# Two 256-column matmuls with the same weights become one of 512 columns, in four stages of a two-block layer

## The reference

```python
# first block
h = rmsnorm(x, norm_mix);  p = h @ w_in
x = x + concat(pool(p), hyena(p), gating(p)) @ w_out          # w_out 2048 x 2048
h = rmsnorm(x, norm_ffn)
up = dwconv3(h @ ffn_w_up, ffn_conv_w, ffn_conv_b)            # 2048 x 11264, width-3 convolution over tokens
gate, val = split(up);  x = x + (silu(gate) * val) @ ffn_w_down   # 5632 x 2048
x = rmsnorm(x, norm_final)
# second block
proj = rms_norm(x) @ w_in_2                                   # attention, RWKV-7, memory attention
merged = sigmoid(ga)*(ya @ w_up_a) + sigmoid(gb)*(yb @ w_up_b) + sigmoid(gc)*(yc @ w_up_c)
return x + merged @ w_o                                       # w_o 2048 x 2048
```

## Time and profile before

| | |
|---|---|
| median of 3 runs | 2539.17 us (2537.14 to 2540.28) |
| span of the profiled execution | 2537.8 us; its own whole time is not listed apart, the median lies 1.4 us above this span |
| mean granted TensorE clock | 0.985 of full speed |
| TensorE busy | 2455.0 us, 97% |
| weight loads busy | 2413.6 us, 95% |
| VectorE busy | 1534.1 us, 60% |
| ScalarE busy | 1185.9 us, 47% |
| DMA | 400.39 MB, mean 158 GB/s |

### The profile page before, as it was taken

How to read it: one execution, slowest core, us unless ns; L and a number is a source line. 1 busy time by engine, 2 the same in 40 slices (tenths; PEclk the granted TensorE clock), 3 DMA queues, 4 the chain that set the end, 5 groups by cost and what they waited for, 6 DMA issues and landing times.

```text
span 2537.8 us, 51128 instructions
## 1 busy us (share of the span) xinstructions
PE 2455.0 (97%) x19960; PEld 2413.6 (95%) x19960; DVE 1534.1 (60%) x2050; ACT 1185.9 (47%) x1502; POOL 12.8 (1%) x27
## 2 busy tenths in 40 slices
PE   6999998999999999997899999999999999999999
PEld 6898997999999999996899999999999999999999
DVE  6456566666555666566866666766576454544454
ACT  5343335665434666434444445444465443434433
POOL 0000000000000000000000000000000000000000
PEclk9999898999999999998999999999999999999999
DMA  6353354555554555554333333333355355555554
GB/s 233 130 180 116 129 187 132 188 170 194 183 186 167 183 181 189 179 185 147 117 119 112 109 120 111 119 123 104 118 175 173 125 184 179 185 176 175 184 187 160
DMA packets 110145, 400.39 MB, mean 158 GB/s; under 512 B 12394, under 2 KB 12421, under 8 KB 109904
## 3 DMA queue, kind: packets, MB, share of 16 engines
q1 hardware_dynamic: 108000, 391.00, 46.4%
q0 software_dynamic: 2032, 7.67, 0.9%
HBM read 396.52 MB, written 2.10 MB: 157 GB/s over the span
## 4 chain that ended last, share of the span: by engine, by line
PE 92%; DVE 5%; issue 1%; ACT 1%; DMA 0%; DVEq 0%; SPq 0%; ACTq 0%
PE bank L417 91%; DVE w_lo L1316 1%; ACT w_hi L909 1%; DVE scratch L1365 1%; PE bank L611 0%; DVE s_k L1365 0%; DVE h_lo L1362 0%; DMA x<-in_xT 0%; DVE cum L1362 0%; DVE root L1404 0%; DVE ping L1362 0%; DVE s_t L1362 0%; DVE qr L1807 0%; DVE acc L1362 0%; DVE s_t L1369 0%
## 5 line engine op out<-in xcount | busy, mean ns | idle before, releaser
L1316 DVE TENSOR_TENSOR w_lo<-raw,w_hi 128x1024 fp32r<-128x1024 f32 x736 | 892.0, 1224 | 803.8 <-ACT w_hi L909 797.5
L909 ACT ACTIVATE w_hi<-raw 128x1024 fp32r<-128x1024 f32 x736 | 770.7, 1057 | 1018.7 <-PE bank L417 999.5
L417 PE MATMUL bank<-h_hi,w_hi 128*128 128x256 f32 x4016 | 1163.3, 290 | 36.6 <-DVE h_lo L1362 15.0
L417 PE MATMUL bank<-h_lo,w_hi 128*128 128x256 f32 x4016 | 1141.0, 284 | 0.0
L417 PE MATMUL bank<-h_hi,w_lo 128*128 128x256 f32 x4016 | 1140.8, 284 | 0.0
L417 PEld LDWEIGHTS bank<-h_hi,w_hi 128*128 128x128 f32 x4016 | 775.6, 193 | 47.0 <-issue 24.4
L417 PEld LDWEIGHTS bank<-h_lo,w_hi 128*128 128x128 f32 x4016 | 775.9, 193 | 3.3 <-issue 2.2
L417 PEld LDWEIGHTS bank<-h_hi,w_lo 128*128 128x128 f32 x4016 | 775.0, 193 | 0.0
L417 PE MATMUL bank<-m_hi,w_lo 128*128 128x256 f32 x704 | 197.8, 281 | 0.0
L417 PE MATMUL bank<-m_hi,w_hi 128*128 128x256 f32 x704 | 197.1, 280 | 0.0
L417 PE MATMUL bank<-m_lo,w_hi 128*128 128x256 f32 x704 | 195.7, 278 | 0.0
(11 more groups left out here) (414 smaller groups left out, 2820.2 us busy)
## 6 DMA issues: line engine op xcount, KB each, us to landing
raw<-in_units SPq DMA_DIRECT2D x736, 512.0 KB, 3.4
x<-in_xT SPq DMA_DIRECT2D x4, 512.0 KB, 5.8
memx<-in_memT POOLq DMA_DIRECT2D x4, 512.0 KB, 7.2
out_y<-obuf SPq DMA_DIRECT2D x8, 256.0 KB, 4.3
bias_t<-in_bias POOLq DMA_DIRECT2D x8, 192.0 KB, 2.9
dft<-in_dft POOLq DMA_DIRECT2D x1, 1024.0 KB, 7.6
decay<-in_decay POOLq DMA_DIRECT2D x1, 768.0 KB, 5.6
con<-in_con SPq DMA_DIRECT2D x1, 546.0 KB, 7.8
```

What stands on the lines that cost most here:

```text
L417: return pe.matmul(out, lhsT, rhs, start=start, stop=stop, skip_group_check=True)
L909: return act.activation(out, in_, ACT.Copy, scale=scale)
L1316: dve.tensor_tensor(w_lo[slot][:, :, :], raw[slot][:, :, :], w_hi[slot][:, :, :].bitcast(F32), ALU.subtract).then_inc(split_done, 1)
```

## The change

In the four stages the high and the low half of an activation now lie in one tensor ("both", with an index 0 or 1 ahead of the tile index). TensorE streams both halves, 512 columns, in one matmul with w_hi into a whole bank: 256 columns of w_hi·hi beside 256 columns of w_hi·lo. The w_lo·hi product, 256 columns, is added into the first half of the bank. A triple becomes a pair. An output tile now fills a bank, a group two banks ("wide"), and all eight banks serve as four wide ones. Whoever evicts has to add the two halves of each bank. As wide group 0 covers banks 0 and 1, and wide group 1 banks 2 and 3, TensorE waits ahead of w_out and ahead of w_o until banks 0 and 1 have both been read.

```diff
-        banks = [ctx.enter_context(nc.psum_tensor(f"bank{i}", [P, 512], F32)) for i in range(8)]
+        wide = [ctx.enter_context(nc.psum_tensor(f"wide{i}", [P, 2, 2 * T], F32)) for i in range(4)]
+        banks = [wide[i // 2][:, i % 2, :] for i in range(8)]
...
+        h_both = sb("h_both", [P, 2, KT, T], F32R)
+        h_hi, h_lo = h_both[:, 0], h_both[:, 1]
...
+        def part_of(b, s):
+            return WIDE[b][:, :, s * T:(s + 1) * T]
...
+            def wide_unit(bank, k0, both, first, last):
+                slot = next(slots) % RING
+                pe.wait_ge(split_done, n.next("split"))
+                for kk in range(UK):
+                    for t in range(2):
+                        o = WIDE[bank][:, t, :]
+                        mm(o, w_hi[slot][:, kk, t * P:(t + 1) * P], both[:, :, k0 + kk, :], first and kk == 0, False)
+                        m = mm(o[:, 0:T], w_lo[slot][:, kk, t * P:(t + 1) * P], both[:, 0, k0 + kk, :], False,
+                               last and kk == UK - 1)
+                m.then_inc(unit_used, 1)
...
+            for b in (0, 1):
+                pe.wait_ge(bank_read[b], n.now(("fill", b)))
             with n.loop(4, {("fill", 0): 1, ("fill", 1): 1, "split": 8}):
-                group(1, y_hi, y_lo, ready=(dve_for_pe, (most, most, most, rest)))
-                group(0, y_hi, y_lo)
+                wide_group(1, y_both, ready=(dve_for_pe, (most, most, most, rest)))
+                wide_group(0, y_both)
...
+                        u = conv_u[:, q, :, :]
+                        to_dve(copy(u, part_of(b, 0)))
+                        act.wait_ge(bank_read[b], n.now(("fill", b)))
                         for s in range(2):
-                            m = act.activation(o[:, s, :], p2(b)[:, s, :], ACT.Identity,
+                            m = act.activation(o[:, s, :], u[:, s, :], ACT.Identity,
...
-                read(tt(dst, t, p2(b), ALU.add), b)
+                step(tt(dst, t, part_of(b, 0), ALU.add))
+                settle()
+                read(tt(dst, dst, part_of(b, 1), ALU.add), b)
...
+                        u = conv_u[:, q, :, :]
                         from_act()
                         n.next(("fill", b))
-                        last = taps([o[:, s, :] for s in range(2)], b, [col("ffn", base + 4 * s) for s in range(2)],
+                        read(tt(u, u, part_of(b, 1), ALU.add), b)
+                        own_bank(b)
+                        from_act()
+                        last = taps([o[:, s, :] for s in range(2)], u, [col("ffn", base + 4 * s) for s in range(2)],
...
+                        t = x[:, 4 * q + 2 * s:4 * q + 2 * s + 2, :]
+                        step(tt(t, t, part_of(b, 0), ALU.add))
+                    settle()
+                    for s, b in enumerate((1, 0) if q % 2 else (2, 3)):
                         n.next(("fill", b))
                         t = x[:, 4 * q + 2 * s:4 * q + 2 * s + 2, :]
-                        read(tt(t, t, p2(b), ALU.add), b)
+                        read(tt(t, t, part_of(b, 1), ALU.add), b)
```

More of the change, by code:

```diff
@@ L248, in build @@
         conv_m = place("conv_m", [P, 2, T], 66 * K)
+        conv_u = place("conv_u", [P, 2, 2, T], 72 * K)
         root2 = place("root2", [P, T], 70 * K)
@@ L432, in unit, with wide_group @@
                 m.then_inc(unit_used, 1)
+            def wide_unit(bank, k0, both, first, last):
[8 more added lines that the diff above has]
+                m.then_inc(unit_used, 1)
+            def wide_group(bank, both, units=4, ready=None):
+                pe.wait_ge(bank_read[bank], n.now(("fill", bank)))
+                n.next(("fill", bank))
+                for u in range(units):
+                    if ready:
+                        pe.wait_ge(ready[0], ready[1][u])
+                    wide_unit(bank, UK * u, both, u == 0, u == units - 1)
             def group(bank, hi, lo, k0=0, units=4, tiles=2, filled=True, arriving=False, ready=None):
@@ L587, in _ @@
                             for t in range(4):
-                                o = p2(pair[t // 2])[:, t % 2, :]
+                                o = WIDE[pair[t // 2]][:, t % 2, :]
                                 wh, wl = wh4[:, kk, t * P:(t + 1) * P], wl4[:, kk, t * P:(t + 1) * P]
[L590 to L593, removed]
+                                mm(o, wh, m_both[:, :, 2 * u + kk, :], u == 0 and kk == 0, False)
+                                m = mm(o[:, 0:T], wl, m_both[:, 0, 2 * u + kk, :], False, u == 10 and kk == 1)
                         m.then_inc(unit_used, 1)
@@ L872, in _ @@
             final_fill.update({b: n.now(("fill", b)) for b in (0, 1)})
+            for b in (0, 1):
+                pe.wait_ge(bank_read[b], n.now(("fill", b)))
             with n.loop(4, {("fill", 0): 1, ("fill", 1): 1, "split": 8}):
-                group(0, mg_hi, mg_lo, ready=(merged_ready, (6, 6, 6, 8)))
-                group(1, mg_hi, mg_lo)
+                wide_group(0, mg_both, ready=(merged_ready, (6, 6, 6, 8)))
+                wide_group(1, mg_both)
         @block.sync
@@ L1429, in _, with taps @@
             normalised(x, lambda t: col("norm_mix", t), scratch, h_hi, h_lo, root, with_units=True)
-            def taps(dst, b, w0, w2):
-                o = p2(b)
+            def taps(dst, o, w0, w2):
                 for s in range(2):
@@ L1445, in hyena @@
                 n.next(("fill", b))
-                last = taps([dst[:, j + s, :] for s in range(2)], b, [col("hy_w", 2 * p + s) for s in range(2)],
+                last = taps([dst[:, j + s, :] for s in range(2)], p2(b), [col("hy_w", 2 * p + s) for s in range(2)],
                             [col("hy_w", 36 + 2 * p + s) for s in range(2)])
@@ L1614, in _ @@
                     par[:, COL["norm_g"]:COL["norm_g"] + KT], ALU.mult))
-            with n.loop(4, {"unit": 8, ("fill", 0): 1, ("fill", 1): 1, "step": 4}) as i:
+            with n.loop(4, {"unit": 8, ("fill", 0): 1, ("fill", 1): 1, "step": 6}) as i:
                 for q, b in enumerate((1, 0)):
@@ L2008, in _ @@
                     dve.wait_ge(merged_ready, n.next("merged"))
-            with n.loop(3, {"unit": 8, ("fill", 0): 1, ("fill", 1): 1}) as i:
+            with n.loop(3, {"unit": 8, ("fill", 0): 1, ("fill", 1): 1, "step": 2}) as i:
                 for b in (0, 1):
@@ L2015, in _ @@
             dve.wait_ge(unit_used, UNITS)
-            read(tt(obuf[:, 14:16, :], x[:, 14:16, :], p2(1), ALU.add), 1)
+            step(tt(obuf[:, 14:16, :], x[:, 14:16, :], part_of(1, 0), ALU.add))
+            settle()
+            read(tt(obuf[:, 14:16, :], obuf[:, 14:16, :], part_of(1, 1), ALU.add), 1)
 SHAPES = {"units": (UNITS, P, UK * UN), "xT": (P, KT, T), "memT": (P, KT, T), "par": (P, NPAR),
```

37 lines of the change are left out of this document (18 added, 19 removed).

## The result

| | before | after |
|---|---|---|
| median of 7 runs each, us | 2539.17 (2536.89 to 2540.68) | 2546.25 (2544.81 to 2548.82) |
| span of the profiled execution, us | 2537.8 | 2543.3 |
| TensorE matmul records | 19960 | 17336 |

The ratio after/before is 1.0028, interval 1.0018 to 1.0039: slower by about 7 us. Forecast were 2522.6 us, between 2506 and 2538. The direction was wrong, and the time lies outside the range.

The account below looks back on a forecast made before the run. TensorE was taken as the bound in all four stages. Gains of 23.9 (pairs) and 4.0 us (FFN up) less 11.3 lost made 16.6 us gained: span 2521.2, median 2522.6 us, range 2506 to 2538.

Parts of the forecast that it names:

- The pair: In w_out, w_o and FFN down a pair takes 333.6 ns, 19.7 less than a triple: 23.9 us gained over 152 units.
- the 11 ns are a price of every matmul: Rival: every matmul pays 11 ns whatever its length, pair 342 ns, gain 6 us, 2533 us; chance 0.17.
- the layout in two stretches: Rival: columns from two stretches 16 KB apart slow the long matmul to 235.6 ns, no pair gains, 2550 us; chance 0.12.
- the new waits: Pauses for bank reads at w_out, w_o and between FFN halves, clock after them, extra adds at stage ends: 11.3 us lost.
- The rule of the Trainium skill: For any matmul, columns at 2.4 GHz plus 2.5 ns: 109.2 ns for 256 columns, 325 for the pair.
- The round: In FFN up, ScalarE's and VectorE's work from one group's last split to the next's: lengthened to 23.0 us for two groups.
- the 4 us at the ends: In FFN up, only first and last groups run at TensorE's new pace: about 2 us gained each half, 4 in all.
- fast end for this round: In FFN up, no handover cost and shorter add and conv_o: 22.2 us for two groups, some 20 us gained in all.
- boundary: Between the FFN's halves TensorE waits for bank 1, now read by VectorE's third add: 1.3 us more.
- the clock at w_out: Lower granted clock after the new pause at the start of w_out: 0.7 us lost, ends 0 and 1.4.
- the chance of 0.73 for faster: Whole kernel: chance, summed over forecast and rivals, that it gets faster by more than about 5 us.

Follow-up runs that it names:

- Experiment 7: Changed kernel plus rows of matmuls behind its last product (256, 512 in one stretch, 512 in two, 384, 128 columns, float32), at rest and beside other engines: 2654.54 us.
- experiment 1: Changed kernel with the high and low halves of an activation tile side by side, so the 512 columns are one stretch: 2546.94 us, ratio 1.0039.
- experiment 2: Changed kernel without the w_lo product in every pair (part of the computation missing): one run, 2455.86 us.
- experiment 8: Changed kernel with ScalarE's inner FFN up loop written out, TensorE and VectorE keeping their loops: 2530.06 us, ratio 0.9956 against the kernel before.
- experiment 10: The kernel before the change with only ScalarE's FFN up loop written out: 2539.88 us, ratio 0.9999.
- experiment 4: Changed kernel with w_out and w_o summing in banks 4 to 7, without the waits for banks 0 and 1: 2538.73 us, ratio 0.9997.
- experiment 3: Changed kernel with the w_lo product over 128 of its 256 columns (part of the computation missing): one run, 2539.03 us.
- experiment 5: Changed kernel with FFN up put back to triples and its old eviction: 2547.45 us, ratio 1.0033.

## Why the prediction was wrong, step by step

- **The pair: this step failed.** "I take the 512-column matmul at 215.8": it takes 228 in the pair and 233 by itself. The gain is 353.3 - 346 = 7 ns a pair, not 19.7: over the 152 units x 8 pairs some 8.9 us instead of 23.9 (8.1 by the stages' own times). FFN down bears it out: 44 units took 2.35 us less, 2.6 by this sum. The price came from float32 rows, read as two passes over the columns at the rate of fp32r. Experiment 7 shows both kinds side by side: 216 ns for a float32 record of 256 columns and 117 for an fp32r one, 233 for an fp32r one of 512. The float32 record is faster than an fp32r matmul over the 512 columns that it was taken for, so its small excess over a round number said nothing of fp32r. The kind to read was the one at hand, at its own pace of 117.8 for 256 columns.
- **The rival nearest in size** was "the 11 ns are a price of every matmul", pair 342, 2533 us. Its mechanism falls too, by experiment 7: the price goes with the columns. It should then have been a rival of its own: 512 columns at twice today's 117.8, which I had only under the layout in two stretches. That rival's number, 235.6, was close to the truth (233), and its reason wrong (experiment 1 and the third row of 7). The prediction said that it decides from about 226 ns up, and at the measured 228 it did: the pairs of the 152 units gained less than the new waits cost.
- **The rule of the Trainium skill**, TensorE: Matmul & The Clock Gate, section Back-to-back issue gap, gives columns at 2.4 GHz plus 2.5 ns for one matmul by itself. The fp32r rows do not agree with it: 117 ns measured for 109.2, and 233 for 215.8; it fits no row of experiment 7 of that type. The measurement decides.
- **FFN up: the mechanism was right, the gain was not there.** The round was forecast at 23.0 us for two groups and is 23.24. Experiments 2, 8 and 10 show that it is the bound after the change and not before. With 0.2 us more in each loop iteration (11 x 0.24 a half) the 4 us at the ends were eaten up. By the stage differences the first half lost 1.4 us and the second 0.9: together 2.3 us lost for 4 forecast gained. The prediction's fast end for this round was also added up wrongly: no handovers, 0.65 for the add and 0.85 for conv_o make the round 0.54 shorter, not 0.4. The measured round was longer than forecast, so that end did not come about.
- **The new waits were right.** Forecast 11.3 us. Measured: w_out 2.10 and 1.6 for the clock, w_o 3.49 and 1.7 (90.1 less the 88.4 of experiment 4), boundary 1.3, the pauses behind w_out and the FFN 0.7 and 1.3, the end 0.8: 13.0. Only the clock at w_out was put too low for this execution, 0.7 for 1.6. But that cost comes and goes. Seven profiled executions have the pause at w_out, and the half level follows it in four (the changed kernel, experiments 1, 3 and 7) and not in three (2, 5 and 8; there w_out takes 88.7 us in 5 and 8). At w_o it follows in six of seven. On the mean that is 4/7 of 1.6, 0.9 us, so the forecast of 0.7 was not far off; in this execution it came out dear.
- **The sum by the measured terms**: with the stages' own times, 4.7 us for the two FFN downs and 1.7 each for w_out and w_o at full clock, it is 8.1 - 2.3 - 13.0, so 7.2 us lost; 7.1 were measured by the medians. That they meet so closely is partly luck, as the clock's share differs from one execution to the next.
- **The range** left out the one rival in which the pairs gain nothing (2550 us, chance 0.12), and it was left out for its reason, the layout; its outcome came by another. With the pair at its measured 346 and everything else as forecast the sum is 8.9 + 4.0 - 11.3 = 1.6 us gained, no change: the chance of 0.73 for faster rested on one unmeasured rate.

Open are why an fp32r column costs 0.456 ns, why the long matmul takes 228 ns ahead of a short one and 233 ahead of its like, why the same pairs take 346.7 ns in one half of the FFN and 353.3 in the other (experiment 8), and whether the clock that took back experiment 5's gain was the edit's doing.

## What to carry to other kernels

Before counting on fewer and longer matmuls, take the pace of the same type by start to start at two lengths: if it goes with the columns, merging gives almost nothing, here 7 ns in 353. Charge each new bank wait with the pause, and with the stretch at the lower clock behind it; here another bank gave both back (7.5 us). When an edit moves work onto helper engines, compute their round against the main engine's: what was hidden there, table loads in each loop iteration, can then be worth more (16 us) than the edit itself. And when an effect of a few us is sought in one trace, compare the stretches at 1.2 GHz first.

## What the runs showed of the hardware

- fp32r streams at 0.456 to 0.460 ns a column at a granted clock of 1.00, for 256, 384 and 512 columns at rest, and for 512 also beside DMA, ScalarE and VectorE work (233 ns; experiment 7). In the kernel itself a 256-column one takes 117.8 ns in FFN down and 120.0 in FFN up.
- A matmul of 128 columns with a weight load of its own takes about 112 ns, not the 58 of its columns; from 256 to 512 columns the time doubles (117 to 233 ns), so no part of it is seen that would be the load's.
- A pause of 2.10 us at w_out was followed by five pairs at 1.2 GHz, and one of 3.49 us at w_o had about 1.1 us of pairs at full clock and then a stretch at 1.2 GHz, granted 0.61 over 4 us in both windows. Neither is certain: behind the pause at w_out the clock stayed at 1.00 in three of seven profiled executions, behind that at w_o in one of seven. Without the pause neither occurs (experiment 4).
- ScalarE loaded a function table, 1.28 us, twice in each iteration of a hardware loop: 44 loads in the FFN. With the loop written out, the same instructions needed 4 (experiment 8).
